# Routing a mixture of experts by token tile, with the first expert outside the loop, in a two-layer decoder trunk

## What is computed

```python
def swiglu(u, w_gate, w_up, w_down):
    return (jax.nn.silu(u @ w_gate) * (u @ w_up)) @ w_down

def moe_swiglu(u, w_router, b_router, w_gate, w_up, w_down):
    ...
    logits = tok.astype(f32) @ w_router.astype(f32) + b_router.astype(f32)
    top_val, top_idx = lax.top_k(logits, TOP_K_EXPERTS)
    gates = jax.nn.softmax(top_val, axis=-1)
    combine = jnp.einsum('tk,tke->te', gates, jax.nn.one_hot(top_idx, N_EXPERTS, dtype=f32))
    out = jnp.zeros((bn * s, d), f32)
    for e in range(N_EXPERTS):
        out = out + combine[:, e:e + 1] * swiglu(tok, w_gate[e], w_up[e], w_down[e]).astype(f32)
```

## Time and profile before

| what | value |
| --- | --- |
| median of 3 runs | 1637.91 us (1637.24 to 1638.79) |
| profiled execution, whole | 1632.35 us |
| profiled execution, span from first to last instruction | 1630.5 us |
| PE busy in matmuls | 1538.7 us, 94% of the span |
| DVE busy | 1254.6 us, 77% |
| ACT busy | 1048.2 us, 64% |
| mean of the granted clock of TensorE | 0.979 |
| from HBM | 467.98 MB, 288 GB/s over the span |
| first expert matmul | 608.94 us |

### The profile page before, as it was taken

How to read it: one execution, slowest core, us unless ns; L and a number is a source line. 1 busy time by engine, 2 the same in 40 slices (tenths; PEclk the granted TensorE clock), 3 DMA queues, 4 the chain that set the end, 5 groups by cost and what they waited for, 6 DMA issues and landing times.

```text
span 1630.5 us, 22147 instructions
## 1 busy us (share of the span) xinstructions
PE 1538.7 (94%) x7571; PEld 1195.2 (73%) x7572; DVE 1254.6 (77%) x1707; ACT 1048.2 (64%) x1381; POOL 62.8 (4%) x90
## 2 busy tenths in 40 slices
PE   4999989999799969999999999999999999999997
PEld 2645468887675458888888888888888888888885
DVE  6896345543682249899899889889989989989987
ACT  3105444443548437787788788788788778778775
POOL 5351000000000000000000000000000000000000
PEclk9999999999899969999999999999999999999998
DMA  9625876544458458999999999999989999999960
GB/s 321 239 104 199 317 283 212 178 179 166 150 178 309 156 219 308 348 353 359 337 356 351 367 340 343 367 334 348 379 321 352 364 332 367 348 337 362 357 255 27
DMA packets 203752, 469.68 MB, mean 288 GB/s; under 512 B 5108, under 2 KB 11558, under 8 KB 203574
## 3 DMA queue, kind: packets, MB, share of 16 engines
q1 hardware_dynamic: 202656, 466.80, 78.8%
q0 software_dynamic: 400, 1.09, 0.3%
q10 hardware_dynamic: 646, 1.16, 0.2%
HBM read 467.98 MB, written 1.05 MB: 288 GB/s over the span
## 4 chain that ended last, share of the span: by engine, by line
PE 81%; ACT 5%; DVE 4%; issue 2%; ACTq 0%; DVEq 0%
PE ps L810 23%; PE ps L812 22%; PE ps L811 22%; PE ps L816 2%; PE ps L1370 2%; DVE w_lo L1949 2%; PE ps L1329 2%; PE ps L1083 1%; ACT work L1845 1%; PE ps L835 1%; ACT uT L1601 1%; ACT w_hi L1588 1%; ACT uT L1610 1%; PE ps L1439 0%; PE ps L1440 0%
## 5 line engine op out<-in xcount | busy, mean ns | idle before, releaser
L1949 DVE TENSOR_TENSOR w_lo<-ring,w_hi 128x1024 fp32r<-128x1024 f32 (+2 forms) x572 | 668.0, 1200 | 118.1 <-ACT w_hi L1588 99.0
L1588 ACT ACTIVATE w_hi<-ring 128x1024 fp32r<-128x1024 f32 (+2 forms) x572 | 595.4, 1045 | 215.2 <-PE ps L812 211.8
L810 PE MATMUL ps<-w_hi,e_hi 128*128 128x512 f32 x896 | 356.6, 398 | 9.7 <-DVE w_lo L1949 9.7
L812 PE MATMUL ps<-w_hi,e_lo 128*128 128x512 f32 x896 | 350.5, 391 | 0.0
L811 PE MATMUL ps<-w_lo,e_hi 128*128 128x512 f32 x896 | 349.6, 390 | 0.0
L1949 DVE TENSOR_TENSOR w_lo<-ring_more,w_hi 128x1024 fp32r<-128x1024 f32 x192 | 228.9, 1222 | 40.5 <-ACT w_hi L1588 38.1
L1588 ACT ACTIVATE w_hi<-ring_more 128x1024 fp32r<-128x1024 f32 x192 | 201.6, 1067 | 70.7 <-PE ps L812 70.7
L810 PEld LDWEIGHTS ps<-w_hi,e_hi 128*128 128x128 f32 x896 | 168.9, 189 | 46.3 <-DVE w_lo L1949 13.2
L812 PEld LDWEIGHTS ps<-w_hi,e_lo 128*128 128x128 f32 x896 | 168.5, 188 | 36.7
L811 PEld LDWEIGHTS ps<-w_lo,e_hi 128*128 128x128 f32 x896 | 169.0, 189 | 33.5
L810 PE MATMUL ps<-w_hi,eT_hi 128*128 128x512 f32 x448 | 176.5, 394 | 5.7 <-DVE w_lo L1949 5.7
(11 more groups left out here) (283 smaller groups left out, 1600.4 us busy)
## 6 DMA issues: line engine op xcount, KB each, us to landing
ring<-in_moe_w_gate SPq DMA_DIRECT2D x48, 2048.0 KB, 10.0
ring<-in_moe_w_up SPq DMA_DIRECT2D x40, 2048.0 KB, 10.2
ring<-in_moe_w_down SPq DMA_DIRECT2D x32, 2048.0 KB, 10.4
ring<-in_w_ada SPq DMA_DIRECT2D x24, 2048.0 KB, 9.3
ring_more<-in_moe_w_down SPq DMA_DIRECT2D x24, 2048.0 KB, 7.9
ring_more<-in_moe_w_up SPq DMA_DIRECT2D x16, 2048.0 KB, 10.3
ring_more<-in_moe_w_gate SPq DMA_DIRECT2D x8, 2048.0 KB, 9.6
ring<-in_ff_w_gate SPq DMA_DIRECT2D x5, 2048.0 KB, 7.8
```

The lines of the kernel that those rows point to most:

```text
L810: mm(o, xh, wh, start=start, stop=False)
L812: return mm(o, xl, wh, start=False, stop=stop)
L1588: fn(w, src, ACT.Copy).then_inc(hi_ready, 1)
L1949: V.tensor_tensor(w_lo[0:n, c, 0:f], src, w_hi[0:n, c, 0:f].bitcast(F32), ALU.subtract).then_inc(lo_ready, 1)
```

## The change

The router runs tile by tile: `router(0)` stands between the last projection and the norm of tile 1, each tile has its own bank and its own signal, and DVE routes each tile on its own. The constants, memsets and token numbers are written before the routing. The position products of tile 0 don't wait for tile 1, and the counts go to another bank behind the positions. The selection of expert 0 follows the positions directly; counts, `comb` and `info` come behind it, with a semaphore `info_first` ahead of the info product. ACT converts all of gate block 0 of expert 0 ahead of the exponential, and DVE splits it between the selection and the slots, in the order chunk 0, 1, slots half 0, chunk 2, slots half 1, chunk 3. `slots_in`, `slots_high` and `slots_low` of expert 0 go half by half, and PE waits for each half of `e_lo` at chunk 0 and chunk 2 of gate block 0. The two bank clears and the zero `selT` follow on DVE. On ACT and DVE expert 0 is written out ahead of the loop, which becomes `Fori(1, E)`; on PE the loop is as before. The job tables are made on DVE between expert 0 and the loop.

```diff
@@ SP
-            sp.wait_ge(router_done, 1)
+            sp.wait_ge(router_done, 2)
@@ PE
-                    w = mm(ps[4][:, t * E:(t + 1) * E], uT[:, k, t * P:(t + 1) * P], w_r[:, k, :],
+                    w = mm(ps[4 + 2 * t][:, 0:E], uT[:, k, t * P:(t + 1) * P], w_r[:, k, :],
...
             pending[0] = 2
+            pe.wait_ge(late_in, 16 * 2)
+            router(0).then_inc(router_done, 1)
             norm(3, 1)
-            pe.wait_ge(late_in, 16 * 2)
-            router(0)
             router(1).then_inc(router_done, 1)
+            member = lambda t: rt[:, t, 16:24]
             pe.wait_ge(member_ready, 1)
-            member = lambda t: rt[:, t, 16:24]
             mm(ps[5][:, 0:E], tri, member(0), start=True, stop=True)
-            mm(ps[5][:, E:2 * E], tri, member(1), start=True, stop=False)
-            mm(ps[5][:, E:2 * E], ones, member(0), start=False, stop=True)
-            mm(ps[5][:, 2 * E:3 * E], ones, member(0), start=True, stop=False)
-            mm(ps[5][:, 2 * E:3 * E], ones, member(1), start=False, stop=True).then_inc(pos_done, 1)
-            def gather(g):
+            mm(ps[5][:, E:2 * E], ones, member(0), start=True, stop=False)
+            pe.wait_ge(member_ready, 2)
+            mm(ps[5][:, E:2 * E], tri, member(1), start=False, stop=True).then_inc(pos_done, 1)
+            mm(ps[4][:, 2 * E:3 * E], ones, member(0), start=True, stop=False)
+            mm(ps[4][:, 2 * E:3 * E], ones, member(1), start=False, stop=True).then_inc(pos_done, 1)
+            def gather(g, first=False):
...
+                if first:
+                    pe.wait_ge(info_first, 1)
...
+                        if kind == "gate" and b == 0 and c % 2 == 0:
+                            pe.wait_ge(e_ready, g * 2 + (c // 2 + 1))
...
-                pe.wait_ge(e_ready, g * 2 + 2)
@@ ACT
+            item_high(moe_c0, 0, moe_fill0[0] + 16, moe_chunk)
             act.wait_ge(gap_ready, 1)
             fn(rt[:, :, 40:41], rt[:, :, 41:42], ACT.Exp).then_inc(gap_exp, 1)
...
-            slots_in(0)
-            slots_high(0)
-            with act.Fori(0, E) as e:
+            for i in range(2):
+                slots_in(0, (i,))
+                slots_high(0, (i,))
+            expert(0, 0, True, True)
+            with act.Fori(1, E) as e:
                 expert(e, e, True)
@@ DVE, the new order (routing)
+            step(V.memset(one_e, 1.0))
+            for t in range(NT):
+                step(V.tensor_copy(info[:, t, 0:1], cst[:, C_TOK + t:C_TOK + t + 1]))
+            for t in range(NT):
+                dve.wait_ge(router_done, t + 1)
+                chained(V.tensor_tensor(lg[:, t, :], ps[4 + 2 * t][:, 0:E], b_r[:, :], ALU.add))
+                chained(V.max(top[:, t, :], lg[:, t, :]))
+                chained(V.max_index(top_i[:, t, :], top[:, t, :], lg[:, t, :]))
+                chained(V.tensor_copy(rt[:, t, 24:26], top_i[:, t, 0:2]))
                 for i in range(2):
                     step(V.tensor_scalar(rt[:, t, 8 * i:8 * i + 8], iota(E), rt[:, t, 24 + i:25 + i], None, ALU.is_equal))
+                step.wait()
+                V.tensor_tensor(rt[:, t, 16:24], rt[:, t, 0:8], rt[:, t, 8:16], ALU.add).then_inc(member_ready, 1)
+            V.tensor_tensor(rt[:, :, 41:42], top[:, :, 1:2], top[:, :, 0:1], ALU.subtract).then_inc(gap_ready, 1)
+            dve.wait_ge(member_ready, 2)
+            dve.wait_ge(pos_done, 1)
+            for t in range(NT):
+                step(V.scalar_tensor_tensor(possel[:, t, 0:E], ps[5][:, t * E:(t + 1) * E], 1.0, rt[:, t, 16:24], ALU.add, ALU.mult))
             step.wait()
+            chained(V.tensor_scalar(possel[:, :, 0:E], possel[:, :, 0:E], -1.0, None, ALU.add))
+            dve.wait_ge(pos_done, 2)
+            for t in range(NT):
+                w = V.tensor_scalar(sel[:, t, :], iota(P), possel[:, t, 0:1], None, ALU.is_equal)
...
+            w.then_inc(sel_ready, 1)
...
+            V.tensor_copy(info[:, :, 1:2], comb[:, :, 0:1]).then_inc(info_first, 1)
+            def job_tables():
...
@@ DVE, into the experts
+            gate_low = lambda *cs: item_low(moe_c0, 0, moe_chunk, cs)
+            gate_low(0, 1)
+            slots_low(0, (0,))
+            gate_low(2)
+            slots_low(0, (1,))
+            gate_low(3)
             step(V.memset(ps[4][:, :], 0.0))
             step(V.memset(ps[5][:, :], 0.0))
...
-            select(0, 0, 0)
-            slots_low(0)
-            with dve.Fori(0, E) as e:
-                step.enter(e, 0, 6)
+            expert(0, 1, 0, True, True)
+            job_tables()
+            with dve.Fori(1, E) as e:
+                step.enter(e, 1, 6)
                 expert(e, e + 1, e, True)
```

More of the change, by code:

```diff
@@ L412, in trunk @@
         jobs = W3.take(3 * E)
+        one_e = bias_rows[:, NT * 48:NT * 48 + E]
+        info_first = sem("info_first")
         final_y = hn
@@ L1441, in scatter @@
                        stop=True).then_inc(scatter_done, 1)
-            gather(0)
+            gather(0, True)
             with pe.Fori(0, E) as e:
@@ L1838, in _, with slots_in @@
             UF = FB * NT
-            def slots_in(g):
-                for i in range(2):
+            def slots_in(g, halves_=(0, 1)):
+                for i in halves_:
                     act.wait_ge(gather_done, g * 2 + (i + 1))
@@ L1847, in slots_in, with slots_high, expert @@
                     w.then_inc(x_e_ready, 1)
-            def slots_high(g):
-                for i in range(2):
+            def slots_high(g, halves_=(0, 1)):
+                for i in halves_:
                     act.wait_ge(x_e_ready, g * 2 + (i + 1))
                     fn(e_hi[:, 4 * i:4 * i + 4, :], x_e[:, 4 * i:4 * i + 4, :], ACT.Copy).then_inc(e_hi_ready, 1)
-            def expert(job, g, gather_next):
+            def expert(job, g, gather_next, gate_made=False):
                 def convert(kind, b, cs=range(NCI)):
@@ L1870, in expert @@
                 for b in range(MB):
[L1871 to L1874, removed]
+                    if b or not gate_made:
+                        convert("gate", b, (0,))
+                        if b == 1:
+                            silu_of(0)
+                        convert("gate", b, (1, 2, 3))
                     if b == 0:
@@ L2327, in _ @@
                 norm_out(3, t)
-            dve.wait_ge(router_done, 1)
-            for t in range(NT):
-                step(V.tensor_tensor(lg[:, t, :], ps[4][:, t * E:(t + 1) * E], b_r[:, :], ALU.add))
             step(V.memset(possel[:, :, E:E + 1], -1.0))
             step(V.memset(comb[:, :, E:E + 1], 0.0))
-            step.wait()
+            step(V.memset(one_e, 1.0))
             for t in range(NT):
-                step(V.max(top[:, t, :], lg[:, t, :]))
-            step.wait()
+                step(V.tensor_copy(info[:, t, 0:1], cst[:, C_TOK + t:C_TOK + t + 1]))
@@ new lines, in _ @@
+            chained(V.tensor_scalar(possel[:, :, 0:E], possel[:, :, 0:E], -1.0, None, ALU.add))
+            dve.wait_ge(pos_done, 2)
+            for t in range(NT):
+                w = V.tensor_scalar(sel[:, t, :], iota(P), possel[:, t, 0:1], None, ALU.is_equal)
+                if t == 0:
+                    step(w)
+            w.then_inc(sel_ready, 1)
+            cnt, rnd, over = jobs[:, 0:E], jobs[:, E:2 * E], jobs[:, 2 * E:3 * E]
+            chained(V.tensor_copy(cnt, ps[4][:, 2 * E:3 * E]))
@@ L2353, in _ @@
             for t in range(NT):
[L2354 to L2357, removed]
+                step(V.tensor_scalar(comb[:, t, 0:E], rt[:, t, 0:8], rt[:, t, 43:44], None, ALU.mult))
+            step.wait()
             for t in range(NT):
-                chained(V.scalar_tensor_tensor(possel[:, t, 0:E], ps[5][:, t * E:(t + 1) * E], 1.0, rt[:, t, 16:24], ALU.add, ALU.mult))
@@ L2360, in _ @@
[L2360 to L2367, removed]
@@ L2368, in _ @@
-            step.wait()
[L2369 to L2373, removed]
+                step(V.scalar_tensor_tensor(comb[:, t, 0:E], rt[:, t, 8:16], rt[:, t, 44:45], comb[:, t, 0:E], ALU.mult, ALU.add))
+            step.wait()
@@ new lines, in _ @@
+            V.tensor_copy(info[:, :, 1:2], comb[:, :, 0:1]).then_inc(info_first, 1)
+            def job_tables():
+                chained(V.tensor_scalar(over, cnt, OVER + 0.5, None, ALU.is_gt))
+                chained(V.tensor_tensor_scan(rnd, one_e, over, 0.0, ALU.mult, ALU.add))
+                step(V.tensor_copy(job_tab[:, 0:E], cnt))
+                step(V.tensor_copy(job_tab[:, 2 * E:2 * E + 1], rnd[:, E - 1:E]))
+                step.wait()
+                chained(V.tensor_tensor(rnd, rnd, over, ALU.subtract))
+                chained(V.tensor_scalar(rnd, rnd, float(E), None, ALU.add))
+                V.tensor_copy(job_tab[:, E:2 * E], rnd).then_inc(tables_ready, 1)
@@ L2389, in select, with slots_low @@
                 w.then_inc(sel_ready, 1)
-            def slots_low(g):
-                for i in range(2):
+            def slots_low(g, halves_=(0, 1)):
```

(16 more changed lines are left out.)

1 line of the change is left out of this document (removed).

## The result

The changed kernel takes 1628.11 us in the median (1626.01 to 1628.48, 4 runs), the kernel before 1638.24 us beside it (1637.24 to 1638.79, 4 runs): ratio 0.9936, 95% interval 0.9919 to 0.9953, 10.1 us faster, with 7.7 and 13.3 us as the bounds that the interval leaves. Forecast were 1627.6 us and a gain of 10.3 us.

What follows compares the result with a forecast made beforehand. Routing ahead of expert 0 lies wholly on the path, then PE paces experts, DVE the opening. Head start 11.5 less 1.2 for job tables gives 10.3 us: from a median of 1637.91 to 1627.6 us, range 1624.3 to 1632.0.

Steps and rivals of the forecast that it cites:

- The gather's start: Start of expert 0's gather on PE, claimed near 590.4 us where it was 597.83, worth 7.4 us.
- The tile chain: DVE's routing steps for tile 1 alone, claimed 1.4 us, bounds 1.0 and 2.05, where the pair took 2.05.
- The gather: Expert 0's gather on PE, taken as wholly at the low clock: 6.64 us, against 3.57 all high.
- The clock's rival: Clock rises at once under the gather, making it 3.57 us: 3.1 us more gain, 1624.5 us; chance 0.14.
- the first step of 1.8 us: Router by tile: router(0) hidden in PE's wait for the norm, router(1) ending about 586.9, gain 1.8 us.
- The opening: DVE's work from slots half 1 to chunk 1 of gate block 1, expert 0: 13.4 us, ending at 612.5.
- can lose 2 us to the low clock: PE in expert 0's first gate block could run 2 us slower without the opening's end moving.
- What comes back: Job tables on DVE between experts 0 and 1 cost 1.2 us, bounds 0 and 1.26.
- B: Chunk 1 of gate block 1 of expert 1, timed from the last projection's end; gain forecast 10.3 us.
- A: Chunk 1 of gate block 1 of expert 0, timed from the last projection's end; gain forecast 11.5 us.
- The inner range: The likeliest case's own range: 1626.3 to 1629.2 us, for tile chain 1.0 to 2.05, job tables 0 to 1.2.
- each turn of this loop should fetch: Instruction-fetch rule for the expert loop's back branch; the trace disagreed, and one back edge less was claimed to change nothing.

Runs made afterwards that it cites:

- e9: The changed kernel run once more, unedited: median 1627.11 us, ratio 0.9938 to the kernel before.
- e3: The changed kernel with the selection of expert 0 put back behind the gate values (counts, comb, info): 1627.80 us, ratio 0.9934.
- e4: The changed kernel with router(0) put back behind the norm of tile 1: 1628.72 us, ratio 0.9945.
- e2: The kernel before with one edit, expert 0 written out ahead of the loop on ACT and DVE: 1637.34 us, ratio 1.0002.
- e10: The changed kernel with selT, clears and gate chunks reordered on DVE, job tables in DVE's wait in block 4 of expert 0: 1624.88 us, ratio 0.9922.
- e1: The changed kernel with only its routing part; gate block 0 and slots as before, tables and clears under the gather: 1631.34 us, ratio 0.9958.
- e5: The changed kernel with bank, slot_info and selT clears moved on DVE to behind gate chunks 0 and 1: 1626.55 us, ratio 0.9931.
- e7: The changed kernel with one PE wait for both halves of e_lo ahead of gate block 0: 1630.95 us, ratio 0.9958.
- e11: As e10, with DVE converting chunk 1 of gate block 1 ahead of the product of silu and up in every expert: 1620.66 us, ratio 0.9898.

## Why the prediction was right

**The gather's start.** Foretold 14.35 us behind the projection's end, measured 14.80. The tile chain took 1.45 us (1.4 forecast). `router(1)` took 3.60 us and not 3.32, so half of the pair's instructions is a little more than half of its time. `router(0)` was hidden, and at the full clock took 1.85 us. `info_first` and `gap_exp` cost nothing, as said.

**The gather.** Taken as wholly at the low clock, 6.64 us; it took 6.74 here and 6.49 in e9. The windows of the changed kernel:

```profile
599.00:600.00 1.00, 1.00 (x6) 1.00 (x6) 0.00 (x0) 0.97 (x3) 0.00 (x0) 0.50 1.06 412
600.00:601.00 1.00, 1.00 (x11) 1.00 (x9) 0.88 (x2) 0.21 (x2) 0.00 (x0) 0.89 1.04 408
```

The clock's rival (up at once) did not come: the clock came back some 6 us after the gather's start, 20.9 us behind the projection's end. What I missed is that a move of the gather by 1.6 us doesn't move the clock's return. In e3 and e4 it came at 20.4 and 20.8 us, with the gather at 16.46 and 16.37, so the later gather has more of its run at the full rate. That is why the first step of 1.8 us, the router by tile, is worth 0.8 (e4). For the whole change this made little: with the gather 7 us later, in before and e2, the return came at 26.9 and 27.4 us, 5.1 and 5.6 behind the gather's start, where the nine profiles with the gather at 14.80 have 5.2 to 6.2. Their gathers took 6.30 to 6.76 us, those of before and e2 6.27 and 6.49. The shortest of the nine, e10, and that of e2:

```profile
594.36 6.30 PE L1373 MATMUL ps<-cst,work 128*128 128x128 f32 x32 [0.65 <-DVE cst L2362]
```

```profile
602.19 6.49 PE L1370 MATMUL ps<-cst,work 128*128 128x128 f32 x32 [4.67 <-DVE cst L2387]
```

So up to 0.5 us of a gather's length varies from profile to profile at one and the same start, and the 0.39 us of e1 lie within that.

**The opening.** From the second `e_hi` to the end of chunk 1 of gate block 1 I summed 13.4 us of DVE: 603.09 to 616.55, 13.46. The wait of PE at up chunk 0 was forecast at 1.3 us and is 1.40. e5 shows that this list is the pace. The price of the half-wise wait was not weighed, since I took PE to be ahead of DVE there; e7 says that PE's lead is worth 1.95 us. By its sums (2.93 and 1.5, with 2.5 covered) most of that is the low clock, but no run has the late start without the low clock. My line that PE "can lose 2 us to the low clock" was not tested by itself: the gate ran at the full clock in the changed kernel, and in e7 it started late as well.

**What comes back.** 1.2 us were forecast for the job tables, and B - A grew by 1.19. The place was wrong: I put it at chunk 1 of gate block 1 (1.8 us of idle time), and it shows as 0.50 at chunk 0 and short delays behind it, with 0.65 at chunk 1 as before.

**Readings that were wrong.** Two did not reach the sum. An expert does not take 127 us: that is the length of the window in the earlier trace rows. From one expert's chunk 1 of gate block 1 to the next one's it takes 125.6 us, which B - A of before shows and, for experts 1 and 2, this row beside 749.73 in the earlier trace rows:

```profile
875.37 0.50 PE L810 MATMUL ps<-w_hi,e_hi 128*128 128x512 f32 x1 [0.65 <-DVE w_lo L1949]
```

And 624.11 is not the only idle stretch of PE in the first expert. Each expert has one in block 4 as well:

```profile
691.51 0.50 PE L810 MATMUL ps<-w_hi,eT_hi 128*128 128x512 f32 x1 [0.71 <-DVE w_lo L1949]
```

So PE idles some 1.4 us in each expert, all of it for DVE, and e11 takes half of that. That an expert takes its time from PE holds all the same. The inner range does not come out of the two terms that are named for it: a tile chain of 1.0 to 2.05 and job tables of 0 to 1.2 give 1626.0 to 1628.3 us, not 1626.3 to 1629.2.

**Code and weights.** Nothing for the unrolled code (e2). The changed kernel and e2 list three packets of the smaller instruction queue from 750 to 1550 us, where before had none, with no idle time of PE that before lacks. The prediction's "each turn of this loop should fetch" takes it that a turn is longer than what an engine holds of its code. No row shows that, and the earlier trace rows counts only 119 instructions of DVE and 112 of ACT at work in a turn, so the packets that are missing there decide nothing. There is no wait of PE for a transfer; an expert keeps its 125.6 us.

In sum A gained 48.07 - 37.28 = 10.8 us (11.5 forecast), B 9.6 (10.3 forecast), the medians 10.1. The 0.7 too much is 0.45 at the gather's start and the rest in its length and in the step to `e_hi` (0.64 us, not 0.57). That the median's gain came within 0.2 us of the forecast is luck: the profiled execution from which it was carried over was an early one, and two medians of the changed kernel differ by 1.0. What the runs bear out is the sum at A and B, to 0.7 us of some 10.

## What to carry to other kernels

Behind a serial stage the engine that prepares operands, and not the one that multiplies, may set how much of a head start is kept: list what it still owes from the last signal on, and move what nobody needs yet into its earlier waits (1.6 us here for the clears, 2.3 with the gate chunks as well). A short piece of bookkeeping is free or not by its place: the same 1.26 us cost 1.2, 0.8 and nothing. And compare profiles from a common event near the edit, since start and tail of two executions of one kernel differed here by more than single steps gave.

## What was not expected of the hardware

Two gathers that started 1.6 us later were shorter: 5.92 us at 16.37 us behind the projection's end and 5.68 at 16.46, where nine at 14.80 took 6.30 to 6.76, the same 32 instructions. The granted clock came back 20.0 to 21.0 us behind the projection's end in all eleven, so 0.4 to 1.1 us of the later start was given back. That is no rule for longer ways: at 21.79 us, in before and e2, the gathers took 6.27 and 6.49 us, and the clock came back at 26.9 and 27.4. What sets the place of the return stays open. These places are read from windows like this one of e3, in which the clock was low for 0.28 us and high for the rest:

```profile
599.00:600.00 1.00, 1.00 (x9) 1.00 (x9) 0.00 (x0) 0.81 (x3) 0.00 (x0) 0.86 1.04 406
```

The clock fell in PE's idle 2.82 us in e7 and did not fall in the 1.40 us in the changed kernel. The time ahead of the change varied from 576.05 to 580.99 us over thirteen profiles of kernels that are alike there, and the tail behind B by about 1 us.
